# Zero products ahead of the first input, query weights in two loads, and the second query tile moved forward

## The reference, cut to what matters

```python
for l in range(DEPTH):                       # DEPTH = 2
    h = rms_norm(x, norm_g[l])
    proj = h @ w_in[l]
    (q, k_c, v_c, k_s, v_s, k_w, v_w, g_lin, z_nsa, u_lru, z_lru, glu_a, glu_b,
     z_conv) = jnp.split(proj, split_points(), axis=-1)
    q = apply_rope(q.reshape(B, T, N_HEADS, HEAD_DIM), cos, sin)
    ...
    x = x + mixed @ w_out[l]
```

## Time and profile before

| what | value |
|---|---|
| median of 3 runs (lowest to highest) | 1367.55 us (1366.68 to 1369.48) |
| the profiled execution: its own time, its span | 1367.13 us, 1365.8 us |
| TensorE (PE) busy, share of the span | 1039.5 us, 76% |
| VectorE (DVE) busy, share of the span | 877.8 us, 64% |
| ScalarE (ACT) busy, share of the span | 477.6 us, 35% |
| GpSimd (POOL) busy, share of the span | 296.5 us, 22% |
| mean rate of transfers | 286 GB/s |

### The profile page before, as it was taken

How to read it: one execution, slowest core, us unless ns; L and a number is a source line. 1 busy time by engine, 2 the same in 40 slices (tenths; PEclk the granted TensorE clock), 3 DMA queues, 4 the chain that set the end, 5 groups by cost and what they waited for, 6 DMA issues and landing times.

```text
span 1365.8 us, 16696 instructions
## 1 busy us (share of the span) xinstructions
PE 1039.5 (76%) x5833; PEld 585.4 (43%) x5833; DVE 877.8 (64%) x2221; ACT 477.6 (35%) x1321; POOL 296.5 (22%) x268
## 2 busy tenths in 40 slices
PE   7998999999899989999988786676453445443435
PEld 4776756477575646445534431232221112211211
DVE  5488643428865444855576798568777766777655
ACT  2013523101352431366357654434233232222312
POOL 0000000000000000000034444446533353433443
PEclk9999999999999999999989898766566666666657
DMA  8362454426337313135389999999999999999997
GB/s 306 123 234 94 141 229 139 185 92 228 131 124 293 117 63 137 62 130 188 125 335 426 414 427 426 426 427 425 428 426 426 427 426 426 426 425 426 427 427 316
DMA packets 56165, 391.05 MB, mean 286 GB/s; under 512 B 9995, under 2 KB 13118, under 8 KB 16018
## 3 DMA queue, kind: packets, MB, share of 16 engines
q0 software_dynamic: 37504, 268.45, 46.7%
q1 hardware_dynamic: 18578, 121.54, 24.2%
HBM read 387.87 MB, written 1.05 MB: 285 GB/s over the span
## 4 chain that ended last, share of the span: by engine, by line
DMA 24%; PE 17%; DVE 11%; ACT 4%; issue 3%; POOL 2%; another core or an unknown queue 1%; ACTq 0%; DVEq 0%
DMA e_uv<-in_experts_dram,e_listed 22%; PE bank L168 16%; DVE e_uv L2918 4%; POOL e_uv L3133 2%; DMA e_uv<-in_experts_dram,e_listed_uv 2%; ACT e_diag L229 1%; ACT L229 1%; PE bank L173 1%; DMA m_w<-in_ada_dram 1%; ACT m_W L229 1%; DVE m_ctx L184 0%; DVE e_hot L184 0%; DVE e_hot L2847 0%; DVE e_h2q L196 0%
## 5 line engine op out<-in xcount | busy, mean ns | idle before, releaser
L3133 POOL DMA_INDIRECT e_uv<-in_experts_dram,e_listed x252 | 283.0, 1123 | 1040.4 <-DVE e_listed L201 800.7
L168 PE MATMUL bank<-e_uv,e_diag 128*32 128x512 f32 x1024 | 231.6, 885 | 279.7 <-ACT e_diag L229 257.8
L2918 DVE CUSTOM_DVE_ANT_0 e_uv<-e_uv,e_h2q 128x1024 f32<-128x1024 f32 x192 | 230.3, 1224 | 107.0 <-DMA e_uv<-in_experts_dram,e_listed 92.6
L168 PEld LDWEIGHTS bank<-e_uv,e_diag 128*32 128x32 f32 x1024 | 40.9, 139 | 404.2 <-ACT e_diag L229 289.3
L168 PE MATMUL bank<-hT,weights 128*128 128x256 f32 x640 | 141.0, 380 | 2.8 <-DVE hT L190 1.4
L168 PEld LDWEIGHTS bank<-hT,weights 128*128 128x128 f32 x640 | 120.8, 190 | 21.0 <-DVE hT L190 1.6
L229 ACT ACT_TABLE_LOAD x79 | 101.4, 1283 | 6.8 <-PE bank L168 1.0
L168 PE MATMUL bank<-weights,hT 128*128 128x512 f32 (+1 forms) x256 | 102.6, 557 | 1.5 <-DVE hT L190 1.5
L229 ACT ACTIVATE e_act<-e_dot 128x4 f32<-128x4 f32 (+1 forms) x81 | 16.6, 205 | 234.9 <-DVE e_dot L2918 220.7
L196 DVE SCALAR_TENSOR_TENSOR conv<-ubuf,vec,conv 128x256 f32<-128x256 f32 x240 | 96.8, 480 | 0.6
L2918 DVE CUSTOM_DVE_ANT_0 e_uv<-e_uv,e_hT 128x1024 f32<-128x1024 f32 x64 | 76.8, 1223 | 22.5 <-DMA e_uv<-in_experts_dram,e_listed 20.1
(11 more groups left out here) (388 smaller groups left out, 1416.4 us busy)
## 6 DMA issues: line engine op xcount, KB each, us to landing
weights<-in_ada_dram SPq DMA_DIRECT2D x8, 2048.0 KB, 8.5
weights<-in_layer_out_dram SPq DMA_DIRECT2D x6, 2048.0 KB, 8.3
e_w_pq<-in_w_pq_dram SPq DMA_DIRECT2D x12, 1024.0 KB
weights<-in_layer_cmp_dram SPq DMA_DIRECT2D x4, 2048.0 KB, 8.3
weights<-in_layer_q_dram SPq DMA_DIRECT2D x2, 2048.0 KB, 8.5
weights<-in_layer_kvc_dram SPq DMA_DIRECT2D x2, 2048.0 KB, 12.7
weights<-in_layer_gb_dram SPq DMA_DIRECT2D x2, 2048.0 KB, 15.6
weights<-in_layer_ga_dram SPq DMA_DIRECT2D x2, 2048.0 KB, 15.3
```

The source lines that it names most:

```text
L168: ins = self.engine.matmul(out, lhsT, rhs, start=start, stop=stop, **kw)
L2918: dve.mark(c.nc.vector.tensor_tensor_reduce(u, u, h2q[tt][n], 1.0, 0.0, MUL, ADD, m["dot"][:, j:j + 1]), ("dots_set", g, c0) if n == c1 - ...
L3133: ins = c.nc.gpsimd.indirect_dma_start(out=to, out_offset=None, in_=rows, in_offset=bass.IndirectOffsetOnAxis(ap=of, axis=0))
```

## The change

TensorE multiplies `cond["sT"]`, which VectorE has filled with zeros, into held bank 4: four products of 128x256 ahead of the turned gain, four between it and the turning of x tile 0, one behind that. VectorE fills `sT` first rather than last. The query weights are loaded in two parts of 1 MB, with x tile 1 between them. `q` of tile 0 is done in two halves of four steps: the first waits for the first part of the weights and the first half of `hT`, the second for the rest; x tile 1 is turned between them. `q` of tile 1 and its rotation on VectorE move from behind `ga` to a place right behind those of tile 0. Layer 1 is as before.

```diff
+    def zeros_multiplied(times):
+        zeros = cond["sT"].rearrange("p k s -> p (k s)")
+        for _ in range(times):
+            pe.mm(O[0][:, 0:2 * P], zeros[:, 0:P], zeros[:, 0:2 * P])
+
+    def first_queries():
+
+        view, landed = weight(m, 0, "q")
+        bank = take("q", 0, 0)
+        for half, event in enumerate((("q_start_in", 0), landed)):
+            if half:
+                x_turned(c, m, K, 0, 1)
+            pe.wait_ge(*at(*event))
+            pe.wait_ge(*c.taken("xT", 0, 0, half))
+            for k in range(4 * half, 4 * half + 4):
+                pe.mm(bank[:, :], hT[:, k, 0:P], view[:, k, :], start=k == 0, stop=k == KT - 1,
+                      tell=filled("q", 0, 0) if k == KT - 1 else None)
+
     if l == 0:
+        pe.wait_ge(*at("sT_zeroed", 0))
+        zeros_multiplied(4)
         gain_turned(c, m, K, 0)
+        zeros_multiplied(4)
         x_turned(c, m, K, 0, 0)
-        pe.wait_ge(*c.taken("xT", 0, 0, 1))
-        by_token("q", 0)
-        x_turned(c, m, K, 0, 1)
+        zeros_multiplied(1)
+        first_queries()
+        pe.wait_ge(*c.taken("xT", 0, 1, 1))
+        by_token("q", 1)
         by_token("kvc", 0)
         pe.wait_ge(*at("constants_in", 0))
...
-    by_token("q", 1)
+    if l:
+        by_token("q", 1)
     by_token("kvc", 1)
...
 def first_vector_start(c, m, K):
     dve, at = c.dve, c.at
+    dve.fill(m["cond"]["sT"], 0.0, tell=("sT_zeroed", 0))
     for name in ("bd", "ubuf", "lbuf", "blk"):
         dve.fill(m[name], 0.0, tell=("bd_zeroed", 0) if name == "bd" else None)
-    dve.fill(m["cond"]["sT"], 0.0, tell=("sT_zeroed", 0))
...
         queries(0)
+        queries(1)
         compressed_rotated(0)
...
-    queries(1)
+    if l:
+        queries(1)
     taps_after("q", 1)
...
-    load_weights(c, first, A, 0, "q")
+    view, landed = weight(first, 0, "q")
+    view, half = view.rearrange("p k n -> p (k n)"), KT // 2 * WIDE
+    c.sp.load(view[:, 0:half], A["layer0_q"][:, 0:half], "q_start_in", 0)
     c.sp.load(x[:, 1, :], rows[:, 1, :], "x1_in", 0)
+    c.sp.load(view[:, half:], A["layer0_q"][:, half:], *landed)
```

## The result

The changed kernel took 1369.44 us (median of 17 runs, 1366.32 to 1372.6) against 1367.55 us (17 runs, 1365.96 to 1369.61) of the kernel before: a ratio of 1.0016, 95% interval 1.001 to 1.0023. That is 1.9 us slower: the interval leaves out 1, the difference is less than the 0.2% that I called the grain of the measurement, and the time is inside the range on record. The profiled execution took 1369.44 us with a span of 1368.1. Runs of one kernel scatter by 3 to 6 us, so single profiles have to be read for places, not for their spans.

The account below looks back on a forecast made before the run. TensorE was taken to fill the first half of the span and transfers the second, so early shifts reach the end. A start gain of 1.4 us less a 1.8 us wait gave 0.4 us slower: 1368.0 us, range 1365.2 to 1371.0.

Parts of the forecast that it names:

- the grain of the measurement: About 0.2%, 2.7 us of the whole time: what a measurement of this kernel can tell from no change.
- The start: Opening up to gb: queries start 1.2 us late but run 2.6 us shorter at the fast clock, gaining 1.4 us.
- all this: Split query weights, halves and x tile 1 turned between them: costed at nothing, with 0 to 0.3 us for the seam.
- the queries start at 12.7 with half of `hT`: First queries: wait for zeros, turning and half of VectorE's copies, so start at 12.7 us rather than 11.49.
- Zeros release the clock: Opening: zero products should raise TensorE's clock as well as data do, at about 10.0 us.
- 5.0 us from the first dense products to the rise: Opening: the clock rises 5.0 us after dense products begin, about 10.0 us; 8.4 if early, 13.4 if late.
- Covers: Opening loads: weight parts and x tile 1 land before use; tile 1 normed 0.9 us ahead; kvc lands 7 us ahead.
- The wait at `posT`: Behind ga: TensorE stands still 1.8 us until VectorE empties the bank of kvw tile 0, which posT takes.
- nothing behind gives it back: After posT: VectorE's later idle times let VectorE, not TensorE, catch up, so all 1.8 us go to the end.
- the clock falls at the new wait: Rival: behind the pause before posT the clock falls and hits ulru, costing 1.7 us, 1369.7 us in all; chance 0.15.
- the fall of the earlier trace: Second block of the kernel before: clocks of 0.69, 0.50 and 0.96 over 2 us each, priced at 1.7 us.
- 23 dense us just before: Before the pause at posT: TensorE's 23 us of dense work, held to speak against the clock falling there.
- the shift would be the same at 300 and at 700 us: Past the first attention steps: everything 0.4 us later than before, equally at 300 and 700 us.

Follow-up runs that it names:

- the second series: The changed kernel run again with no edit, six runs: median 1371.72 us, ratio 1.003 to the kernel before.
- Zeros alone: Only the nine zero products and the earlier fill of sT, put on the kernel before: 1367.62 us, ratio 1.0.
- halves alone: The changed kernel without zero products and with tile 1's queries where they were: 1365.94 us, ratio 0.9996 to the kernel before.
- moved only: Only the query product and rotation of tile 1 moved, on the kernel before: 1371.66 us, ratio 1.0031.

## Why the prediction was right in sign, and where it wasn't in size and cause

**The forecast** was 0.4 us slower, within the grain; it is 1.9, a time of 1369.44 us instead of 1368.0. That it lies in the range is partly luck: the second series had a median of 1371.72, above the range's 1371.0. What the runs give for the terms:

- *The start, a gain of 1.4 us (0.1 lost to 2.2 won)*: 2.2, 1.1 and 1.6 in three profiles. The size was right, by luck; the cause was not. I put all of it to the zero products and costed "all this", the halves and the split load, "at nothing". Zeros alone move `gb` by 0.1 us the wrong way, halves alone by 1.4 us the right way (in a profile with an early rise). "At nothing" also left out that the second half of the queries hides VectorE's copy of x tile 1, 1.81 us in moved only. The step that failed is the one that has the queries start at 12.7 with half of `hT` as part of the price of the zeros: that half belongs to the other edit, which by itself starts them at 10.52.
- *Zeros release the clock*: right. The records of the granted clock begin at 7.9, 10.4 and 9.1 us in the three profiles, against 16.6 and 17.4 in the two of the kernel before, and the pace agrees: the second eight zero instructions took 1.83, 2.69 and 1.98 us from start to start, at 0.43 or 0.22 each. That zeros serve as data do, as the Trainium skill's Part 1 ("TensorE: Matmul & The Clock Gate") leads one to think, the trace bears out. I took 5.0 us from the first dense products to the rise; 3.1, 5.7 and 4.3 were seen with zeros, 3.1 to 6.0 from the first query in the kernels without.
- *Covers*: x tile 1 was squared at 9.80 (9.9 forecast), the rest of the query weights made no wait, `kvc` neither.
- *The wait at `posT`, 1.8 us*: 1.86, 1.85 and 1.86. The argument from the bank order and VectorE's fixed work held to a tenth. That nothing behind gives it back was right but for a nuance: without the wait, VectorE takes 0.9 of it back by itself further on, so the bank is worth 0.8 us and not 1.8.
- *The rival "the clock falls at the new wait", 1.7 us at a chance of 0.15*: its size was right (1.7 us measured; the fall of the earlier trace rows from which I took it cost the kernel before only 0.8, since TensorE had waits there), its chance too low by what the profiles show. It stood in two of the three profiles of the changed kernel, and in moved only. An estimate from the three profiles: the start 1.6 won, the wait 1.86 lost, and 1.7 in two of three executions make -1.6 + 1.86 + 1.1 = 1.4 us slower, which covers most of what lies between 0.4 and 1.9. The step that failed is the weighing of "23 dense us just before" against the pause: with dense products before it in all five profiles, the clock fell behind the pause in three.
- *The remaining half microsecond* is within the scatter. The falls at 474 and 556 us in the first profile, 2.1 and 0.5 us, lie far from the change; I can't show that the change makes them more frequent.

The prediction also said that the shift would be the same at 300 and at 700 us. In the first profile it wasn't, because of those falls: 0.24 us ahead at 300, about 1.7 behind at 700.

## What to carry to other kernels

Warming an engine is only worth what it doesn't push back: nine zero products, four of them ahead of ready input in an in-order queue, cost what they won, while five, four of them done about when the input was ready, won 1.6 us in a profile where no weights were late, and starting on half of the input was worth 1.4 us in another. When work is moved off one engine's stretch, redo the sum for its partner in that stretch: 6.9 us of TensorE's work left and 2.75 of VectorE's did; VectorE's own waits (1.5) and TensorE's slack (0.9) took up part of the difference, and 1.86 us came back as a wait for a PSUM bank. And a pause of TensorE of two microseconds between small turns should be priced with its clock, or filled: filled with products of constants, the clock stayed up in its one profile and the median was 1.3 us lower, in intervals that overlap.

## What the runs showed of the hardware that I hadn't expected

The granted clock fell behind a pause of 1.86 us in three of five profiles that had it, about 0.5 to 1.3 us after its end, and came back 3 to 4 us later; the changed kernel itself escaped it in one profile and had it in two. What a fall of this length costs depends on where it stands: 1.7 us behind `posT`, where TensorE has no gap, 0.8 at 621 us, 0.5 at 557 us and nothing at 124 us. The moment of the rise at the start moved by 2.5 us between executions of one kernel (7.9, 10.4 and 9.1 us in the changed kernel). So one profile tells too little of the clock. Whether a kernel with a pause scatters more isn't shown: the changed kernel's runs reach from 1366.3 to 1372.6 us, but those of the kernel before, over the series, from 1364.8 to 1371.7.
